# Hybrid encoder block on one core: the value projection moved ahead of the attention heads, and the weight ring of the merge gates cut from five slots to four

## The reference

```
h    = rmsnorm(x) * norm_g
proj = h @ w_in        -> aq, ak, av, ag | cq, ckv, kr, bg | ga, gb
A: 8 heads, differential attention with ALiBi:
   p  = softmax(q1 k1') - lam * softmax(q2 k2');  oa = p @ v;  rmsnorm per head, silu(ag) gate
B: 8 heads, latent attention (q and kv from 512-wide compressed rows, rotary key), silu(bg) gate
out = rmsnorm(x + (sigmoid(ga) * (oa @ w_oa) + sigmoid(gb) * (ob @ w_ob)) @ w_out)
```

## Time and profile before

| | us |
|---|---|
| median of 3 runs | 1503.29 (1502.8 to 1504.59) |
| the profiled execution, its own time | 1504.52 |
| its span, first to last instruction | 1502.7 |
| PE busy in the span | 1463.2 (97%) |
| DVE busy | 959.6 (64%) |
| ACT busy | 582.8 (39%) |
| DMA, mean over the span | 124 GB/s |

### The profile page before, as it was taken

The page is one execution under the profiler, slowest core; times in us unless marked ns, Lnnn a source line. Parts: engine busy times, 40 slices in busy tenths (PEclk is TensorE's granted clock), DMA queues, the critical chain, the costliest instruction groups (busy, mean ns, idle before and its releaser), DMA issues.

```text
span 1502.7 us, 18776 instructions
## 1 busy us (share of the span) xinstructions
PE 1463.2 (97%) x6892; PEld 1218.6 (81%) x6892; DVE 959.6 (64%) x1367; ACT 582.8 (39%) x823; POOL 35.3 (2%) x58
## 2 busy tenths in 40 slices
PE   7699999999999999999999999999999999999997
PEld 6587878887888888888888888888888888888886
DVE  5887889786666666666756547677778354433441
ACT  7544344434434434334433334434444122222331
POOL 0000000000000000000000000000000000000000
PEclk9999999999999999999999999999999999999999
DMA  7558676665322222222223332222232434344532
GB/s 240 196 168 269 194 245 214 192 216 153 110 72 83 72 81 79 75 84 70 81 73 85 85 98 78 64 70 63 70 119 70 152 115 154 116 151 154 154 98 112
DMA packets 183687, 186.85 MB, mean 124 GB/s; under 512 B 19536, under 2 KB 137936, under 8 KB 183120
## 3 DMA queue, kind: packets, MB, share of 16 engines
q1 hardware_dynamic: 179280, 177.72, 39.2%
q10 hardware_dynamic: 4352, 8.39, 1.5%
HBM read 173.49 MB, written 12.58 MB: 124 GB/s over the span
## 4 chain that ended last, share of the span: by engine, by line
PE 91%; DVE 4%; ACT 2%; issue 2%; DMA 1%; POOL 0%; SPq 0%; DVEq 0%; POOLq 0%; ACTq 0%
PE duo L1825 28%; PE duo L1827 27%; PE duo L1826 27%; PE duo L1876 2%; PE duo L1853 1%; PE duo L1850 1%; DVE m_lo L1251 1%; DMA spare<-in_w_in_dram 1%; PE duo L1907 1%; PE duo L1901 1%; PE duo L1872 0%; PE duo L1869 0%; PE duo L1871 0%; PE duo L1868 0%; PE duo L1867 0%
## 5 line engine op out<-in xcount | busy, mean ns | idle before, releaser
L1126 DVE TENSOR_TENSOR w_lo<-w_raw,w_hi 128x1024 fp32r<-128x1024 f32 (+1 forms) x174 | 209.8, 1206 | 281.4 <-ACT w_hi L640 280.5
L1825 PE MATMUL duo<-h_hi,w_hi 128*128 128x512 f32 x784 | 309.3, 394 | 2.0 <-DVE h_lo L1295 1.7
L640 ACT ACTIVATE w_hi<-w_raw 128x1024 fp32r<-128x1024 f32 (+1 forms) x174 | 181.9, 1046 | 331.3 <-DMA w_raw<-in_w_out_dram 97.8
L1827 PE MATMUL duo<-h_hi,w_lo 128*128 128x512 f32 x784 | 305.8, 390 | 0.0
L1826 PE MATMUL duo<-h_lo,w_hi 128*128 128x512 f32 x784 | 305.6, 390 | 0.0
L1825 PEld LDWEIGHTS duo<-h_hi,w_hi 128*128 128x128 f32 x784 | 147.3, 188 | 32.0 <-DVE h_lo L1295 2.1
L1827 PEld LDWEIGHTS duo<-h_hi,w_lo 128*128 128x128 f32 x784 | 147.2, 188 | 31.6
L1826 PEld LDWEIGHTS duo<-h_lo,w_hi 128*128 128x128 f32 x784 | 147.4, 188 | 29.2
L709 ACT ACTIVATE m_hi<-m_raw 128x1024 fp32r<-128x1024 f32 (+2 forms) x65 | 91.4, 1406 | 129.1 <-PE duo L1827 50.6
L1825 PE MATMUL duo<-m_hi,s_hi 128*128 128x512 f32 x256 | 102.1, 399 | 8.9 <-DVE m_lo L1251 8.4
L1251 DVE TENSOR_TENSOR m_lo<-m_raw,m_hi 128x1024 fp32r<-128x1024 f32 (+2 forms) x65 | 107.0, 1646 | 5.0 <-ACT m_hi L709 5.0
(11 more groups left out here) (242 smaller groups left out, 2550.8 us busy)
## 6 DMA issues: line engine op xcount, KB each, us to landing
w_raw<-in_w_in_dram SPq DMA_DIRECT2D x196, 256.0 KB, 3.1
m_raw<-in_w_in_dram SPq DMA_DIRECT2D x64, 512.0 KB, 4.5
m_raw<-in_w_in_dram SPq DMA_DIRECT2D x66, 256.0 KB, 3.4
w_raw<-in_w_out_dram SPq DMA_DIRECT2D x56, 256.0 KB, 3.3
spare<-in_w_in_dram SPq DMA_DIRECT2D x16, 512.0 KB, 4.9
w_raw<-in_w_oa_dram SPq DMA_DIRECT2D x32, 256.0 KB, 3.4
sig<-gates SPq DMA_DIRECT2D x8, 1024.0 KB, 6.9
w_raw<-in_w_ob_dram SPq DMA_DIRECT2D x32, 256.0 KB, 3.3
```

Source lines behind the costliest of these rows:

```text
L640: act.activation(w_hi[:, piece.slot, 0:cols], w_raw[:, piece.slot, 0:cols], ACT.Copy).then_inc(hi_ready, 1)
L1126: dve.tensor_tensor(w_lo[:, piece.slot, 0:cols], w_raw[:, piece.slot, 0:cols], w_hi[:, piece.slot, 0:cols].bitcast(F32), ALU.subtract).the ...
L1825: pe.matmul(dst, lhs_hi, rhs_hi, start=start, stop=False)
L1827: return pe.matmul(dst, lhs_lo, rhs_hi, start=False, stop=stop)
```

## The change

- The values of all eight heads are projected first, token-major (`values`), in 12 steps of 1 MB of weights ahead of the merge gates: 4 steps V0 (first 8 k-tiles, tokens 0 to 255), 4 steps V (the other 8 k-tiles, all tokens) and 4 steps V1 (first 8 k-tiles again, tokens 256 to 511). They are copied out of PSUM by ACT, stored in DRAM (`v_d`, 2 MB) and loaded again head by head (`values_in`).
- The combinations of `h` are formed on DVE during the V steps, from `h_hi + h_lo`, in a buffer of their own, so `h_lo` stays in place and no late split of `h` is left.
- The raw ring of the merge weights has `M_RAW` = 4 slots, none of them in `h`. All four groups consist of X and Y steps.
- A heads have 6 steps, and their extras are spread over 12 places, two for each step (one in its middle). The order of the softmax work on ACT and DVE is new.
- SP loads only pieces 0 to 2 before the end of the merge stage.

```diff
-A_STEPS, C_STEPS, B_STEPS, F_STEPS = 8, 20, 4, 8
+A_STEPS, C_STEPS, B_STEPS, F_STEPS = 6, 20, 4, 8
-M_RAW, M_HI = 5, 3
+M_RAW, M_HI = 4, 3
-PASSES = [("P1", 0, 4), ("P2", 0, 4), ("P1", 1, 4), ("A0", 0, 8), ("B0", 0, 8), ("P2", 1, 4), ("A0", 1, 8), ("B0", 1, 8),
-          ("X", 2, 8), ("Y", 2, 8), ("X", 3, 8), ("Y", 3, 8)]
+V_SPLIT = 4
+PASSES = [("V0", 0, range(V_SPLIT)), ("V", 0, range(V_SPLIT, HALF_K)), ("V1", 0, range(V_SPLIT))]
+PASSES += [(kind, g, range(HALF_K)) for g in range(M_GROUPS) for kind in ("X", "Y")]
...
-TURN_X_AT = {0: (6,), 1: (7,), 3: (8, 9), 4: (10, 11), 5: (12, 13), 6: (14, 15)}
+TURN_X_AT = {0: (6, 7), 2: (8, 9, 10, 11), 3: (12, 13, 14, 15)}
...
+            def values_in(h):
+                if isinstance(h, int) and h == 0:
+                    sp.wait_ge(c11_ready, M_GROUPS)
+                    for out_n in v_out:
+                        sp.wait_ge(out_n, 32)
+                else:
+                    sp.wait_ge(v_lo_ready, h)
+                    sp.nop(nofuse=True)
+                sp.dma_start(v_raw[:, :, :], v_d[:, bass.ds(h * P, P)].rearrange("(t p) c -> p t c", p=P)
+                             ).then_inc(v_in, 16)
...
+                    if s == 3:
+                        values_in(head.h)
...
-            a_head(0, range(SLOTS))
+            a_head(Head(0, 0), range(3))
             sp.wait_ge(m_used, N_MERGE)
...
             def a_step(s, head, cur, prev):
                 if s == 0 and prev:
+                    gate(h - 1, h * A_STEPS, other)
+                    pt_hi(h - 1, 0, TR)
+                    exp_a(h - 1, 2)
+                if s == 1 and prev:
                     pt_hi(h - 1, 1, TR)
                     exp_a(h - 1, 3)
...
             def merge_step(n):
...
+                for j in range(2):
+                    if n == RAW_AT:
+                        whole_of(j)
+                    if n == SUMS_AT:
+                        sums_of(j)
+                    if n == S12_LO_AT:
+                        s12_lo_of(j)
+                    if n == S34_LO_AT:
+                        s34_lo_of(j)
...
             def a_step(s, head, cur, prev, first=False):
                 if s == 0 and prev:
+                    norm_a(h - 1, 1)
+                    pt_lo(h - 1, 0, TR)
+                    max_a(h - 1, 2, first)
+                    gate_copy(h - 1, other)
+                if s == 1 and prev:
                     pt_lo(h - 1, 1, TR)
+                    max_a(h - 1, 3, first)
                     norm_a(h - 1, 2)
...
             def a_extras(q, h, cur, prev):
+                if q == 0 and prev:
+                    scores_a(h - 1, 3, False)
+                    turn_p_a(h - 1, 0)
+                if q == 1 and prev:
+                    turn_p_a(h - 1, 1)
+                if q == 3 and prev:
+                    turn_p_a(h - 1, 2)
+                    pv(h - 1, 0, True)
+                if q == 5 and prev:
+                    turn_p_a(h - 1, 3)
+                if q == 7 and prev:
+                    pv(h - 1, 1, True)
...
+                if q == 9 and cur:
                     scores_a(h, 0, not prev)
+                if q == 10 and cur:
+                    scores_a(h, 1, not prev)
...
+                if q == 11 and cur:
                     scores_a(h, 2, not prev)
```

More of the change, by code:

```diff
@@ L550, in _ @@
                 sp.dma_start(lam_in[:, i, :], src.broadcast_to([P, A_DIM])).then_inc(lambdas_in, 16)
-            a_head(0, range(SLOTS, A_STEPS))
-            with sp.Fori(1, HEADS) as h:
-                a_head(h)
+            a_head(Head(0, 0), range(3, A_STEPS))
+            a_head(Head(1, A_STEPS))
+            with sp.Fori(0, HEADS // 2 - 1) as i:
+                for head in pair_of_heads(i):
+                    a_head(head)
             for b in range(2 * LT):
@@ L719, in unit_hi @@
[L719 to L728, removed]
-                    last = act.activation(h_raw[:, k, HALF_T:SEQ], bank[UNIT_BANK[i]][:, j * HALF_T:(j + 1) * HALF_T],
-                                          ACT.Copy, scale=g_in[:, k:k + 1])
-                last.then_inc(h_raw_ready, 1)
@@ L875, in merge_step @@
                         gate21(g)
-                    if g >= 2 and n == end + 3:
+                    if n == end + 3:
                         gate11(g)
-            for n in range(8, N_MERGE):
+            for n in range(V_SPLIT, N_MERGE):
                 merge_step(n)
@@ L1448, in merge_step @@
                         sum_c21(g)
-                    if g >= 2 and n == SECOND_END[g] + 1:
+                    if n == SECOND_END[g] + 1:
                         sum_c11(g)
-            for n in range(8, N_MERGE):
+            for n in range(V_SPLIT, N_MERGE):
                 merge_step(n)
@@ L1506, in a_step @@
                 if s == 2 and prev:
-                    silu_half(h - 1, 1)
-                if s == 3 and prev:
+                    pt_lo(h - 1, 2, TR)
+                    norm_a(h - 1, 3)
+                if s == 3 and prev:
+                    silu_half(h - 1, 0)
+                    pt_lo(h - 1, 3, TR)
+                    silu_half(h - 1, 1)
+                if s == 4 and cur:
+                    dve.wait_ge(proj_hi, h * 2 + 2)
+                    for m, rows64 in enumerate((LOW, HIGH)):
+                        last = dve.tensor_tensor(ka_lo[rows64, m, :], other[rows64, :], ka[rows64, m, :].bitcast(F32),
+                                                 ALU.subtract)
+                    last.then_inc(acc_read, 1)
+                if s == 4 and prev:
                     dve.wait_ge(o_squared, h)
@@ L1525, in a_step @@
                     max_a(h, 0, not prev)
+                    v_lo(h, v_raw[:, :, :])
+                    max_a(h, 1, not prev)
                 if s == 5 and prev:
@@ L1530, in a_step @@
                                              ).then_inc(o_normed, 1)
+                if s == 5 and cur:
+                    norm_a(h, 0)
+                if s == 5 and prev:
                     dve.wait_ge(o_normed, h)
@@ L1533, in a_step, with a_head @@
                     dve.tensor_tensor(gate_of(h - 1), gate_of(h - 1), oT[:, :], ALU.mult).then_inc(head_gated, 1)
[L1534 to L1545 removed]
+            first_head = Head(0, 0)
             for s in range(A_STEPS):
[L1548 removed]
+                split_lo(first_head.piece(s + AHEAD))
                 merge_step(N_MERGE + s)
[L1550 removed]
+                a_step(s, first_head, True, False)
                 set_up(s)
[L1552 to L1555 removed]
+            def a_head(head, first=False):
                 for s in range(A_STEPS):
[L1557 to L1558 removed]
+                    split_lo(head.piece(s + AHEAD))
+                    a_step(s, head, True, True, first)
+            a_head(Head(1, A_STEPS), True)
+            with dve.Fori(0, HEADS // 2 - 1) as i:
+                for head in pair_of_heads(i):
+                    a_head(head)
             def c_norm(i):
@@ L1882, in turn_p_a @@
                     pe.wait_ge(pt_lo_ready, tile_no(head, t) - 1)
-                elif not first:
+                elif not isinstance(head, int) or head > 0:
                     pe.wait_ge(o_normed, head)
@@ L1889, in turn_p_b, with pv @@
                 turn(e_b[:, t % 2, :], SC[t], p_turned)
-            def pv(head, pair):
+            def pv(head, pair, in_a=False):
+                if in_a and pair == 0 and (not isinstance(head, int) or head > 0):
+                    pe.wait_ge(o_copied, head)
                 pe.wait_ge(pt_lo_ready, tile_no(head, 2 * pair + 1))
```

763 lines of the change are left out of this document (324 added, 439 removed).

## The result

The changed kernel takes **1517.18 us** (median of 4 runs, 1516.03 to 1517.58) against 1503.54 of the kernel before: ratio 1.0086, 95% interval 1.0074 to 1.0098, so 13.6 us slower. Forecast were 1507.5, slower, with a range of 1493 to 1520: the direction held and the result lies in the range, but 1.2 us above the forecast's own case (1501 to 1516), and the size was a third of what came.

The account below looks back on a forecast made before the run. PE was taken to bound everything, with 35.5 us lost in the merge stage. Terms -3.4 - 13.9 + 14.6 + 5.0 + 1.9 = +4.2 gave 1508.7 from the profiled 1504.5, 1507.5 against the median of 1503.3; range 1493 to 1520.

Parts of the forecast that it names:

- forecast's own case: Whole kernel: forecast 1507.5 us, all of it between 1501 and 1516; chance 0.48.
- What bounds, and the value projection: PE bounds everything, 35.5 us lost in the merge stage; moving value matmuls costs 87.1 us each way, zero net.
- The rival by which they stall on `x`: V steps at the start lose 18 us, not 3.6, giving 1522; counted within the slow cases' 0.15.
- The -3.4 of the transposes: A heads: four transposes of `v` per head removed, 8 x 0.43 us, -3.4.
- Tile 2: A heads: a 10.8 us chain against 9.1 us of PE work makes PE wait in every head; +14.6 us.
- The rival by which it would be on time: A heads: tile 2's chain comes under 9.1 us, no wait, total 1493; chance 0.17.
- one split pass out of the chain: A heads: one split pass on either engine leaving the 10.8 us chain would bring it under 9.1.
- no other extra is short by more than tile 2: A heads: everything behind the wait shifts along, and no other extra falls short by more.
- Four slots: Merge groups: reloading four steps ahead makes weights late, 13.2 us lost; bounds 0 and 21.
- The first head: First A head: late keys' low part makes PE wait, +5.0 us, and a halved clock behind it adds +1.9.
- The table load: First A head: priced at the trace row's 1.28 us; the skill's 1.38 us drain would add 1.4 to the sum.
- waits beget waits: Rival: slow loads (+8), repeated clock halving (+1.9 each), longer A waits (+6), about 1523; within the slow cases' 0.15.

Follow-up runs that it names:

- e1: The changed kernel with one swap on DVE: norm_a of tile 2 before max_a of tile 3; 1518.13 us, ratio 1.0107 to the kernel before.
- e5: The changed kernel with norm_a of tile 2 moved to the end of step 0, of tile 3 to the end of step 1; 1505.6 us.
- e6: The changed kernel with the gate stores of groups 0 to 2 cut to 32 of 512 columns; 1512.1 us.
- e7: The changed kernel with byte-cut merge ring, both late norms moved up, head 0's piece 3 loaded early, its value load behind piece 5; 1484.71 us.
- e4: The changed kernel with its merge slots cut by bytes, a ring of 16 units of 2 KB; 1508.84 us, ratio 1.0032 to the kernel before.
- e2: The changed kernel with the value load of head 0 moved behind piece 5; 1510.95 us, ratio 1.0047 to the kernel before.
- e8: The changed kernel with head 0's piece 3 loaded before the merge stage ends and its value load behind piece 5; 1509.07 us.
- e3: The changed kernel with head 0's piece 3 loaded before the merge stage ends, value load kept ahead of piece 4; 1508.67 us.

## Why the prediction was right, and where it was short

- *What bounds, and the value projection*: right. Value steps and turns took 94.3 us for 91.5 of work; 2.8 were lost, 3.6 forecast. The rival by which they stall on `x` fell. The -3.4 of the transposes are in the sum from the heads' start to the mark, which closes to 0.6: -87.1 - 3.4 + 13.8 + 11.8 = -64.9 for -64.3.
- *Tile 2*: right, mechanism and size: eight gaps that are 1.73 us longer than a matmul's cadence, 13.8 for +14.6. The rival by which it would be on time, at 0.17, fell. Its escape ("one split pass out of the chain") was too easy by its own links: a pass is 1.1 us, which leaves 9.7 of the 10.8, still over 9.1. e1 took `max_a`, 1.45 us, out of the chain and the wait moved; e5 shortened two chains. The sentence that no other extra is short by more than tile 2 was right, and hid that the next is short by 0.2 once tile 2 is on time.
- *Four slots*: the mechanism was right, the term was too low: 23.7 lost in the groups for 18.2, the largest miss in us. The late X steps behind the gate stores (X3, X4 and X6 of groups 1 to 3) lost 6.8 where it had 4.2. The turns from X to Y lost 12.0 where it had 10.0. The rest is a late Y6 and small gaps. At group 0 it had 1.0 for the value stores; what came was a wait of 2.2 at the turn, with about 1.7 of half clock behind it. It was not the value stores: the load took 6.6 us (issued at 131.57, DVE takes it up at 138.19), 19 us after the last of them was issued, and in e6 the same turn waits 1.6 and 1.3. A ring that just fits on the landing time of a quiet load pays for each slow one.
- *The first head*: this is the step that was furthest off for its size, **+5.0 and +1.9 where 11.8 came**: 7.0 of waiting, and 4.5 of half clock, which lies beyond the bound of 2 that the prediction gave it. It priced the landing of piece 3 at 3.1 from the median in the earlier trace rows, and named in the same text that loads beside gate stores take 7.9; the last group's stores go out just there. Piece 3 took 7.8 for the 4.0 of the sum, piece 4 another 1.0 more than it had, so the chain is 4.8 later; the low part of the queries is late besides that of the keys, and the clock falls twice. The 16.2 us behind it came out at 15.5.
- *The table load*: the forecast used the row. In the changed kernel ACT waited for the `lam` sum for 4.25 us behind it in any case, so the result doesn't tell the two prices apart.

The case that the prediction called "waits beget waits" (1523, with a second clock fall) came halfway true: loads slower than the median, and three clock falls where the forecast had one. So the mechanisms were right, but both large misses go the same way, and that the result still lies in the range is owed in part to its width: only the upper end of 1520, above the forecast's own 1516, holds it. (The terms of that case add up to at least 17.8 over 1507.5, so 1525 and not 1523.)

## What to carry to other kernels

Price a load by what shares the DMA engines at its place, not by the kernel's median, above all at a seam between stages, where the last stores of one meet the first loads of the next. In a list where one engine prepares step n+2 and finishes step n+1, put what waits for a transfer behind what does not, at least at the steps where the transfer is late. When a wait is taken away, work out the next chain behind it before the edit, and what the edit does to that chain: here tile 3 was 0.2 us from being late, the swap made its chain 1.6 longer, and half the fix gave nothing.

## What the runs showed of the hardware

- A merge load of 768 KB alone lands in 4.4 to 4.8 us, beside gate stores issued from ACT in 5.0 to 7.0, up to 7.9 where loads go out five steps ahead (e7). The transfers of 256 KB that make up a piece, two each, land in 3.2 (median); piece 3, with a gate store beside it and six small loads ahead, took 7.8. The Trainium skill, DMA: Bandwidth & Descriptors, section "Queues, rings and completion order", says that each DMA engine takes turns between the queues it has work for. e6 fits that: with the stores from ACT cut to a sixteenth, the same loads on SP's queue took 4.5 to 5.1. Single loads of 1 MB took 5.9 to 7.1 with no store near (the first three Y loads of group 0 here and in e6, one of group 1 in e6), where others take 5.0 to 5.5; no run says why.
- In the changed kernel, behind the waits of 2.2, 2.8 and 4.2 us matmuls started every 427 ns for 3 to 6 us, which cost about 1.7, 1.7 and 2.8 us on top; behind the eight of 1.6 they did not. The length of the wait alone doesn't decide it: in e4 a wait of 1.8 was followed by half clock, in e7 one of 2.2 at the same Y0 of group 3 was not, nor one of 2.6 in e1. The windows behind the first two (e4, then e7):

```profile
385.40:390.40 5.00, 5.00 (x15) 4.00 (x16) 4.83 (x6) 0.65 (x1) 0.00 (x0) 0.66 0.52 188
385.42:390.42 5.00, 5.00 (x22) 4.11 (x23) 4.83 (x6) 0.60 (x1) 0.00 (x0) 1.00 0.48 183
```

- Between profiles of kernels that are alike there, the four groups went from 326.8 (e2) to 330.1 us (e5) and the value steps from 94.0 (e8) to 98.7 (e3): one profile can't tell 0.2% of this kernel.
